# A split moved behind the norm, and unread products while the norm runs, at the end of an expert stage

## What is computed

```
h = layer_norm(ALPHA * h + mixer(h))          # gated linear attention, then differential attention
h = layer_norm(ALPHA * h + hier_moe(h))       # 16 experts in 4 groups, top 2 of one group
...                                           # twice, layers 0 and 1
x = layer_norm(ALPHA * x + 0.5 * swiglu(x));  x = layer_norm(ALPHA * x + mix(x));  x = layer_norm(ALPHA * x + 0.5 * swiglu(x))
...                                           # second model, twice
```

## Time and profile before

| | us |
|---|---|
| median of 3 runs (lowest, highest) | 1907.75 (1907.04, 1908.02) |
| the profiled execution | 1906.78 |
| its span, first to last instruction | 1905.0 |
| TensorE busy | 1860.3 (98%) |
| VectorE busy | 1295.7 (68%) |
| ScalarE busy | 1006.0 (53%) |
| GpSimd busy | 123.5 (6%) |
| mean granted TensorE clock | 0.986 of full speed |

### The profile page before, as it was taken

One profiled execution on the slowest core, in us unless ns is written; L12 is line 12 of the kernel. 1 busy time (PEld: TensorE's weight loads), 2 busy tenths in 40 slices (PEclk: granted clock), 3 DMA queues, 4 the chain that ended last, 5 costly groups with the idle time before them and its releaser, 6 DMA issues.

```text
span 1905.0 us, 21839 instructions
## 1 busy us (share of the span) xinstructions
PE 1860.3 (98%) x9118; PEld 1549.1 (81%) x9118; DVE 1295.7 (68%) x1313; ACT 1006.0 (53%) x1069; POOL 123.5 (6%) x105
## 2 busy tenths in 40 slices
PE   7999999998999999998999999999999999999998
PEld 6788888887978888886888887888888888778886
DVE  4569999997778898997555657655464545676544
ACT  6446777774646777774443364444344424635431
POOL 1021000001011000000000300100010003020000
PEclk9999999999999999998999999999999998999999
DMA  9447999996435999996555642655565556336551
GB/s 339 152 147 249 358 370 359 357 361 201 145 129 196 370 356 358 357 372 213 179 196 172 214 138 88 202 194 169 188 221 178 177 175 206 120 131 201 184 178 59
DMA packets 220170, 426.56 MB, mean 224 GB/s; under 512 B 7560, under 2 KB 28304, under 8 KB 220064
## 3 DMA queue, kind: packets, MB, share of 16 engines
q1 hardware_dynamic: 214256, 406.91, 62.0%
q0 software_dynamic: 5808, 18.17, 3.0%
HBM read 423.99 MB, written 1.06 MB: 223 GB/s over the span
## 4 chain that ended last, share of the span: by engine, by line
PE 92%; DVE 4%; ACT 2%; DMA 1%; issue 1%; POOL 0%; DVEq 0%; SPq 0%
PE ps L447 26%; PE ps L449 26%; PE ps L448 26%; DVE Wlo L416 2%; PE ps L558 2%; PE ps L2429 1%; PE ps L2399 1%; PE ps L2335 1%; ACT Whi L404 1%; PE ps L1544 1%; PE ps L538 1%; PE ps L537 1%; PE ps L536 1%; PE ps L2415 1%; PE ps L1937 1%
## 5 line engine op out<-in xcount | busy, mean ns | idle before, releaser
L416 DVE TENSOR_TENSOR Wlo<-raw,Whi 128x2048 fp32r<-128x2048 f32 (+2 forms) x387 | 868.3, 2247 | 445.1 <-ACT Whi L404 444.4
L404 ACT ACTIVATE Whi<-raw 128x2048 fp32r<-128x2048 f32 (+2 forms) x393 | 736.3, 1877 | 480.6 <-PE ps L449 476.1
L447 PE MATMUL ps<-Whi,XTh 128*128 128x512 f32 (+2 forms) x1504 | 579.3, 385 | 14.2 <-DVE Wlo L416 8.1
L449 PE MATMUL ps<-Whi,XTl 128*128 128x512 f32 (+2 forms) x1504 | 569.7, 379 | 0.0
L448 PE MATMUL ps<-Wlo,XTh 128*128 128x512 f32 (+2 forms) x1504 | 569.4, 379 | 0.0
L447 PEld LDWEIGHTS ps<-Whi,XTh 128*128 128x128 f32 x1504 | 287.6, 191 | 70.7 <-DVE Wlo L416 9.6
L449 PEld LDWEIGHTS ps<-Whi,XTl 128*128 128x128 f32 x1504 | 286.8, 191 | 52.5
L448 PEld LDWEIGHTS ps<-Wlo,XTh 128*128 128x128 f32 x1504 | 287.4, 191 | 49.8 <-issue 0.5
L447 PE MATMUL ps<-Whi,hTh 128*128 128x512 f32 x352 | 137.7, 391 | 0.0
L449 PE MATMUL ps<-Whi,hTl 128*128 128x512 f32 x352 | 137.1, 389 | 0.0
L448 PE MATMUL ps<-Wlo,hTh 128*128 128x512 f32 x352 | 137.0, 389 | 0.0
(11 more groups left out here) (327 smaller groups left out, 1867.5 us busy)
## 6 DMA issues: line engine op xcount, KB each, us to landing
raw<-in_moe_w_gate SPq DMA_DIRECT2D x64, 1024.0 KB, 5.4
raw<-in_moe_w_up SPq DMA_DIRECT2D x64, 1024.0 KB, 5.5
raw<-in_moe_w_down SPq DMA_DIRECT2D x64, 1024.0 KB, 5.7
raw<-in_ffn_gate SPq DMA_DIRECT2D x44, 1024.0 KB, 5.1
raw<-in_ffn_up SPq DMA_DIRECT2D x44, 1024.0 KB, 5.1
raw<-in_ffn_down SPq DMA_DIRECT2D x40, 1024.0 KB, 5.0
raw<-in_w_in SPq DMA_DIRECT2D x18, 1024.0 KB, 6.4
raw<-in_a_w_in SPq DMA_DIRECT2D x10, 1024.0 KB, 12.3
```

Of the source, the lines that this page charges most:

```text
L404: act.activation(Whi[:, i % NS, 0:m * n], raw[:, i % NR, 0:m * n], ACT.Copy).then_inc(w_rounded, tick(w_rounded, "rounded", i))
L416: dve.tensor_tensor(Wlo[:, i % NR, 0:m * n], raw[:, i % NR, 0:m * n], h.bitcast(f32), ALU.subtract).then_inc(w_rest, tick(w_rest, "rest", i))
L447: pe.matmul(o, xh(k, t), h[:, q, :], start=k == first, stop=False)
L449: x = pe.matmul(o, xl(k, t), h[:, q, :], start=False, stop=k == end)
```

## The change

Three edits.

- `job_dve` gets an argument `upto`, a cap on how far VectorE splits ahead in the step. For the last down product it is `last_unit(v + 1) + 2`, that is L+2. The split of L+3 is then issued by the next `rest_units` that asks for it, in `second_dve`, behind `XTl` of block 1 and ahead of the split of L+4. This holds in both expert stages. ScalarE's rounding of L+3 stays where it is.
- In stage l = 1 TensorE runs a new function `awake_pe` behind the overflow branch, where stage l = 0 has its bias table, and ahead of the transposes of block 0.
- `awake_pe` takes a bank, makes 18 products of `idr` with a view of `mkr` that repeats its 128 columns four times (512 columns), all into the same bank, and frees the bank. Nothing reads them.

```diff
-    def job_dve(dve, name, evac, nt=2, skew=False, hold=0, after=False):
+    def job_dve(dve, name, evac, nt=2, skew=False, hold=0, after=False, upto=NU):
...
             if ahead and not after:
-                rest_units(dve, group[-1] + NS)
+                rest_units(dve, min(group[-1] + NS, upto))
...
         overflow_pe(pe, l, place)
         if l == 0:
             bias_table_pe(pe)
+        else:
+            awake_pe(pe)
         x_turn_pe(pe, v + 1, 0)
+
+    def awake_pe(pe):
+
+        b = bank(pe, "awake")
+        pe.wait_ge(*on("mask"))
+        for _ in range(18):
+            pe.matmul(PS[b][:, :], idr[:, :], bc(mkr[:, 0:1], (0, 4), (1, 128)), start=True, stop=True)
+        free(pe_done, "awake")
...
-                for z in job_dve(dve, name, evac, 1, hold=int((g, hf) == (3, 1))):
+                upto = last_unit(v + 1) + 2 if (g, hf) == (3, 1) else NU
+                for z in job_dve(dve, name, evac, 1, hold=int((g, hf) == (3, 1)), upto=upto):
```

## The result

| | before | after |
|---|---|---|
| median of 18 runs each | 1908.26 | 1902.81 |
| lowest, highest | 1906.66, 1912.01 | 1900.50, 1907.98 |
| profiled execution, span | 1906.78, 1905.0 | 1902.40, 1900.6 |
| mean granted clock of the profiled execution | 0.986 | 0.989 |

The ratio after to before is 0.9972, with a 95% interval of 0.9965 to 0.9978: 5.3 us less (4.2 to 6.7). The forecast was 1901.3, 6.4 us less, and the range 1899.6 to 1905.0. Lines behind the edits are numbered some ten higher now: 1664 for 1654, 1708 for 1698, 1911 for 1900.

A forecast was written before the change was run, and what follows sets the result against it. TensorE, busy 98% of the span, was taken as the bound. Gains of 2.93 us at the first end and 3.49 at the second, 6.4 in all, took 1906.78 to 1900.4, and 0.97 for the median gave 1901.3; range 1899.6 to 1905.0.

The forecast's parts named there:

- `Ygl` waits for the split of L+3, at both ends: Ends of both expert stages: that weight unit's split, not `Ygh`, releases `Ygl`; moving it gains 2.19 and 1.53 us.
- The first end gains 2.19 there: End of the first expert stage: without the second split, `Ygl` can start 2.19 us earlier, at 432.41.
- The clock stays full at the first end, worth 0.74: Line 1900 after the first expert stage: less idling may keep full clock, ending `XTl`'s 0.74 us idle; bounds -1.8 to 0.74.
- 18 products at 0.227, 4.1 us, in the shadow of the norm: Second end: unread products finish at 876.0, delaying transposes 0.47 us, hidden by VectorE's statistics with a thin margin.
- The clock stays full at the second end, worth 1.96: After the second expert stage: the burst keeps 2.4 GHz, so the next 21 matmuls take 4.8 us, not 6.76.
- The stretch at 559.91: Transposes, then 2.17 us idle in the profile before, grant 1.00 in 560 to 564: evidence that such idling keeps the clock.
- The moved split is hidden: Behind `XTl` at both ends: the split of L+3 finishes before TensorE needs it, margin 2.5 us at the second end.
- Both stages behind the ends let the gain through whole: Stages after both ends: TensorE paces them, so the whole 6.4 us reaches the total time.
- the burst gives nothing: Rival at the second end: the clock falls after the burst or before the next products; 1903.3 or 1904.0, chance 0.18.
- the clock falls inside the burst: Rival at the second end: products take 0.43 us each, transposes come 2.5 us later; 1905.4 to 1906.2, chance 0.10.
- slower: Rival at the second end: the 18 products don't overlap, 0.68 us each, 12.2 in all; 1909.8, chance 0.04.
- the split becomes the wait: Rival at one end: the split of L+3 comes up to 2.3 us late for TensorE; 1903.6, chance 0.06.

The follow-up runs named there:

- `split_only`: The change without the 18 unread products, only the split of L+3 moved at both ends, against the kernel before: ratio 0.9985, 2.9 us less.
- `after_again`: The change itself, unedited, run again against the kernel before: ratio 0.9973.
- `burst_only`: The change with the split of L+3 left ahead of `Ygl`, only the 18 unread products kept, against the kernel before: ratio 1.0001.
- `router_burst`: The change plus 9 unread products ahead of the first narrow matmuls of each router, against the kernel before: ratio 0.9995.
- part one: The move of the split of L+3 behind `XTl` at both ends; the change without it, against the kernel before: ratio 1.0001.
- `router_free_burst`: The change, router's narrow products in a bank past the mixer's output sums, 9 unread products ahead in a free bank, against before: 0.9967, median 1902.25.

## Why the prediction was right, and where its sum was off

1. *`Ygl` waits for the split of L+3, at both ends*: shown. At the second end it now starts 868.77, 0.03 us behind `Ygh`; `split_only` gives 1.56 us (forecast 1.53) up to the next stage's first product. The second end as a whole gains only 1.10 by it, since without the burst the half clock that follows lasts longer.
2. *The first end gains 2.19 there*: mis-sized. From the last product, `Ygl` started 2.87 us later before and 1.35 after (434.60 - 431.73, 433.13 - 431.78), a gain of 1.52; in `after_again` 1.97 (432.05 - 431.15). The split of L+3 is gone from there, but `Ygl` still waits for the split of L+2 and starts 0.57 us behind the end of `Ygh`; of the prediction's signs, a start "within 0.1 us of the end of `Ygh` at both ends" failed here, and so did "1.5 us idle ahead of both first scatters" (2.18). The transfers are behind at this end: the split of L+1, at 426.10, waited 1.33 us for ScalarE, and ScalarE for a landing, where it started at 425.36 in the profile before. How late they are changes from one execution to the next: in the eleven profiles with the moved split `Ygl` starts 0.81 to 1.36 us behind the last product. The prediction took this end as paced by the splits alone, at the times of the one profile before.
3. *The clock stays full at the first end, worth 0.74*: shown in the three profiles of the change, line 1900's matmuls 3.70 us (forecast 3.5), `XTl` without idle time. It is worth 0.84 (2.36 in all less 1.52). `split_only` has a grant of 1.00 in 436 to 440 too, `burst_only` 0.60, so it is the moved split that does it. First end in all 2.34 to 2.81 against 2.93. It isn't certain in each execution: in ten of the eleven profiles with the moved split the clock stayed, in that of `router_burst` it fell to 0.78 in 436 to 440 behind 1.96 us of idling, and the first end took 14.10 us.
4. *18 products at 0.227, 4.1 us, in the shadow of the norm*: 4.22 us by starts, 0.234 each. The transposes came 875.02 - 868.10 = 6.92 us behind the last product, forecast 7.1, and `XTl` follows the statistics with no gap, as the forecast's thin margin said.
5. *The clock stays full at the second end, worth 1.96*: shown by the profiles: 4.86 to 4.89 us for the 21 products in all ten with both parts, 6.76 in before and 7.22 in `split_only`. The timed ratios agree (about 2.3 us between `split_only` and the change) but overlap. The ground that the prediction gave for it was weaker than it said. The stretch at 559.91, whose 2.17 us idle "did no harm", is followed by a grant of 0.78 in 564 to 568 in the same profile, a row that it didn't read: the clock did fall behind that idling and the narrow matmuls. That it held at the ends is what the runs showed, not what that stretch showed.
6. *The moved split is hidden*: shown. In the profile after TensorE waits for `Wlo` once, 8.2 us at the start of the program, and the stage between doesn't lengthen in `split_only`.
7. *Both stages behind the ends let the gain through whole*: this step failed for the execution profiled. 1.52 us were given back between the ends, in the router, to a longer stretch at half clock. I had allowed for the clock's moment in the range, not in the sum. The cause of the longer stretch stays open. The three profiles of the change itself have it, the four with 6.8 us are of other kernels. An earlier arrival at the router may make it likelier, or it is chance: the clock's moments vary between executions, and two of the four had the earlier arrival as well.

In place of 2.93 + 3.49 = 6.4 the profiled pair shows 2.36 + 3.45 - 1.52 = 4.3, and the medians 5.4. The forecast's nearness to the medians is thus in part luck: the ends give 5.8 in the profiles, 0.57 less at the first than forecast, and what the stages behind them give back differs between executions.

The rival "the burst gives nothing" is refuted by the 21 products, "the clock falls inside the burst" is what happens without part one, "slower" is refuted at 0.231 us each, and "the split becomes the wait" did not come.

## What to carry to other kernels

Unread products held the clock where they began before it fell (behind 1.50 us of idling) and not where they began with its fall (behind 3.06), so first shorten the idle time ahead of them: here the parts alone gave 0.15% and nothing, and both 0.27%. Count them to end with the work that hides them, since those beyond cost their full length, and check that their PSUM bank is free at that moment, or they wait and then run in the way. With a clock whose falls move between executions, one profile carries some 2 to 4 us of chance in 1900: 1.6 in the stage between, and from the second end to the last instruction 1016.3 to 1019.9 us in kernels that don't differ there. A gain of this size has to be read stage by stage with the half clock beside it.

## What the runs showed of the hardware that was not expected

- Float32 transposes of 128x128 held TensorE's clock at 2.4 GHz: 38 of them in 4.37 us gave the second end (16.15 us) and the time (0.9974) of 18 wide products.
- The same kernel's executions differ in how long the clock is low, and this goes with a good part of their spread. Of the 18 runs of the change, the fastest (1900.5) has a mean grant of 0.990, the slowest (1908.0) 0.986. By the shares, (0.014 - 0.010) x 2 x 1904 is 15 us more at half speed, worth up to 7.6 us (5.7 to 9.5 with the rounding of the shares); the two differ by 7.5. It is not all of the spread: two runs of `after_again`, 1901.36 at 0.989 and 1906.14 at 0.988, are 4.8 us apart, and 0.001 of the clock is worth 1.9, with its rounding at most 3.8.
- The clock can fall while TensorE is busy without a gap, behind a run of 24 matmuls of 20 columns: 0.57 in 576 to 580 before, with 4.00 of 4 us busy, and in `router_free_burst` 0.90 in 560 to 564 with no idle time ahead of the run. It doesn't always: the same run from 128.14 to 130.9 in `router_free_burst` had 1.00. Thinning the narrow matmuls out among wide ones didn't cure it (0.9979).
